# Row buffers, PSUM banks, product order and weight splits of a streaming encoder step

## The chip, the cores and the metric

The kernel runs on one core of one Trainium2 chip. The metric is the device time of one launch in microseconds (us). The kernel before takes 997.57 us, the median of three runs (997.35 to 997.97).

## The reference, cut to what matters

One layer of a hybrid encoder for 512 prompt tokens and 32 sample tokens (544 columns), model width 1024, all in float32:

```
h = rmsnorm(x, g1);  z = h @ w_in            # 1024 -> 8200 columns, split into
#   mq mk mv mo (mLSTM), mi mf, sb sc sx (short conv), dq dk dv (diff attention), gt (3 x 1024 gates)
ya = sigmoid(mo) * rmsnorm(mlstm(mq, mk, mv, mi, mf))
yb = sb * dwconv3(sc * sx)
yc = rmsnorm(diff_attention(dq, dk, dv, cache_k, cache_v)) * 0.8
x  = x + (sum_b sigmoid(gt_b) * (y_b @ w_branch[b])) @ w_out
up = rmsnorm(x, g2) @ w_up                   # 1024 -> 5632
upc = causal_dwconv3(up)
x  = x + (silu(upc[:2816]) * upc[2816:]) @ w_down
y  = rmsnorm(x, norm_f)
```

The outputs are y and the new states (k, v, C, n, m, and the last rows of both convolutions).

## The kernel before, in words

All tensors lie transposed, features on the 128 partitions and the 544 tokens along the free axis. Every large product is done in three passes of 272 columns: ScalarE (ACT) rounds a weight tile of 4 x 128 columns to `w_h` (`split`, L1019), VectorE (DVE) makes the rest `w_l` (`split`, L1315), and TensorE (PE) adds high x high, high x low and low x high. Such a weight tile is a unit. There are five slots for split units (NSPLIT), and the split of unit g + 4 (AHEAD) stands in the queues of ACT and DVE at the place of the block that multiplies with unit g.

The input projection works on pairs of 128-feature blocks: 30 pairs named (mq, 0), (mv, 0), ... (gt2, 3), in the list `pairs`. A pair's 2 x 2 block product (two feature blocks by two token halves) is formed with Strassen's scheme in seven products of 12 matmuls, called 1 to 7 (`strassen_product`, L1788). Products 1, 6, 7, 4 accumulate one after another in one PSUM bank (bank 0 or 2, in turn by pair), and after each of them the running sum is one output block. Product 2 has bank 1, products 5 and then 3 accumulate in bank 3. ACT copies the bank to the row buffer after 1, 6, 7 and 4 (L1141); DVE adds bank 1 after 2 and bank 3 after 5 and after 3 to what ACT copied ("merge", L1496). The next product in a bank waits until the sum before it has been read out. The merge of 5 stands in DVE's queue at the place of 7, since it adds to the block that ACT copies after 7. Some products use weight sums that DVE makes beforehand (`make_t`, L1335, L1339), at places counted back from their use.

The order of all work is one list, ORDER, built by a planner at the top; each engine walks through it and takes what is its own. A counter, `clock`, rises by one for each Strassen product and by two for each branch product. Small steps are hung on it by `at_time` and are put in the list when the clock has come so far: the mLSTM steps ("ml"), the attention steps ("at": scores s, row maximum mx on DVE, exponential ex on ACT, difference of the two maps wd on DVE, transposes t on PE, copy wt on ACT, product with the values o, output transpose y), and the steps after a pair ("post": tanh of a gate, the short convolution's u, w, c, the splits hi and lo of a branch's input). For a pair whose product 1 was already put inside the pair before, the order is 2, 6, 5, 7, next pair's 1, 4, 3. For gate pairs after a gate pair it is 1, 5, 6, 2, 7, branch product, 4, 3, branch product.

A branch product ("pr", 24 matmuls on L1729) multiplies a branch's input with `w_branch`; its two halves need two neighbouring banks, and it waits until DVE has drained the last user of both. DVE drains it with L1651, and adds it to `merged`. The banks are given by `project`: a pair's first branch product gets bank 1 and the chain bank that the pair doesn't use, the second bank 1 and the pair's own. After the last gate pair, and after (gt0, 3), two more branch products follow, in banks 0, 1 and then 2, 3.

Row buffers: the pairs mo, sx, sb and gt are copied to `tmp`, four rows, two for each pair, so two pairs at a time. `tmp_user` lists who must be done with a pair of rows before ACT's copy after product 1 may write it (`wait_tmp_free`). The pair (gt1, 0) follows (sb, 0) on the same rows, and (gt1, 1) follows (sb, 1).

After the branches come w_out (8 blocks "wo"), the second norm, 44 blocks "up" of the FFN with the convolution on DVE (`ups`, `acc`), and w_down ("dn", 6 units of 4 or 3 k-tiles for each output block). After the last "up" block ACT first waits for the last gated product, rounds it (`high_g`, L1028), and only then comes to the splits that stand at the place of the first "dn" block.

Of the kernel before, what the change touches and what calls it, by code (L numbers as in the profile page):

```python
# [50 lines left out]
def streaming_encoder_step(nc, x_prompt, x_sample, cache_k, cache_v, state_C, state_n, state_m, state_conv,  # L51
# [32 lines left out]
    pair_banks = {q: (2 * (i % 2), 1, 3) for i, q in enumerate(pairs)}  # L84
# [59 lines left out]
    def put(pair, w):  # L144
        prod(pair, w)
        if w == 3:
# [17 lines left out]
    pr_banks = {}  # L164
    for i, q in enumerate(pairs):
# [90 lines left out]
    merged_at = {q: max(n_of(q, 5), n_of(q, 7)) for q in pairs}  # L256
    for kind, a, n in ORDER:
        if kind == "p":
            pair, w = a
            if w in (1, 6, 7, 4):  # L260
                count["act"] += 1
                drained[n] = ("act", count["act"])
            if w in (2, 3) or n == merged_at[pair]:
                count["dve"] += 1
                drained[n_of(pair, 5) if n == merged_at[pair] else n] = ("dve", count["dve"])
# [28 lines left out]
    for kind, a, n in ORDER:  # L294
# [9 lines left out]
        else:  # L304
            for b in banks_of[n]:
                last_user[b] = n
# [66 lines left out]
    tmp_row, tmp_before, holder = {}, {}, [None] * 4  # L373
# [14 lines left out]
    for kind, a, n in ORDER:  # L388
# [10 lines left out]
        elif kind == "p" and a[1] == 1:  # L399
# [10 lines left out]
            elif q[0] == "gt1":  # L410
                tmp_user(q, "merged_added", 2 * q[1] + 2, rows=2)
# [7 lines left out]
    with ctx:  # L419
# [120 lines left out]
        u_c = at(28672, "u_c", [P, 2, TW + 2])  # L540
# [34 lines left out]
        for nm in (  # L575
# [27 lines left out]
                "x_used u_ready cu_ready conv_kept "  # L603
# [23 lines left out]
        def wait_tmp_free(eng, key):  # L627
            for name, v in tmp_before[key]:
# [5 lines left out]
        def tmp_pair(key):  # L634
            return tmp[:, tmp_row[key]:tmp_row[key] + 2, 0:T]
# [18 lines left out]
        def dst_of(pair, blk, half):  # L654
# [8 lines left out]
            return tmp[:, tmp_row[pair] + blk, cols]  # L663
# [73 lines left out]
        def units(n):  # L737
            return range(first_unit[n], first_unit.get(n + 1, len(UNITS)))

# [239 lines left out]
        def _(act):  # L979
# [56 lines left out]
            for kind, a, n in ORDER:  # L1036
                if n is not None:
                    for g in units(n):
                        if g + AHEAD < len(UNITS):
# [84 lines left out]
                elif kind == "p" and a[1] in (1, 6, 7, 4):  # L1124
                    q, w = a
                    blk, half = {1: (0, 0), 6: (1, 0), 7: (1, 1), 4: (0, 1)}[w]
# [144 lines left out]
                elif kind == "up":  # L1271
# [834 lines left out]
```

## Time and profile before

| what | value |
|---|---|
| median of 3 runs | 997.57 us |
| the profiled execution's own time | 997.3 us |
| its span | 995.5 us |
| PE busy | 971.8 us (98%) |
| DVE, ACT, POOL busy | 692.2, 472.6, 163.9 us |
| DMA, mean over the span | 100 GB/s |
| granted TensorE clock | 1.00 in the stages looked at |

The span is the profiler's, from the first to the last instruction; the time has 1.8 us more around it. A timeline row says start, duration, engine, line, operation and tiles, and in square brackets how long the engine had been idle before it and what released it. The end of a matmul is modelled and overlaps with the next one.

### The profile page before, as it was taken

The page shows a single profiled execution, that of the slowest core. Times are in us where ns is not written, and L with a number is a line of the kernel's source. Part 1 is how long each engine was busy: PE and PEld are TensorE (multiplying, and loading weights), DVE is VectorE, ACT ScalarE, POOL GpSimd, SP SyncE. Part 2 cuts the span into 40 slices and gives each one's busy share as a digit, 9 for nine tenths or more (in the row PEclk, how much of TensorE's full clock was granted, in tenths as well). Part 3 has the DMA queues.
Part 4 walks back from the last instruction along what each step waited for, and adds up shares of the span by engine and source line. Part 5 has one row for each costly group of instructions (what it writes and reads, how often), then busy time and mean ns, then how long its engine had stood idle before and what let it go on. Part 6 is the DMA issues. An engine that isn't in the chain of part 4 may idle for free.

```text
span 995.5 us, 20106 instructions
## 1 busy us (share of the span) xinstructions
PE 971.8 (98%) x7749; PEld 948.7 (95%) x7749; DVE 692.2 (70%) x1161; ACT 472.6 (47%) x982; POOL 163.9 (16%) x346
## 2 busy tenths in 40 slices
PE   7999999999999999999999999999999999999996
PEld 6999899999999998899999999999999999999996
DVE  6887666687667898777775557777777777634354
ACT  5675555576555665665554323333333333322242
POOL 2000121110121221021112212111111111111011
PEclk9999999999999999999999999999999999999999
DMA  6522243364231222223245212222222222332242
GB/s 197 196 85 86 72 112 108 91 210 135 66 86 43 86 86 85 65 86 107 64 129 174 86 45 91 93 93 93 91 92 86 86 86 80 120 97 81 81 147 97
DMA packets 104086, 99.87 MB, mean 100 GB/s; under 512 B 4868, under 2 KB 99481, under 8 KB 103735
## 3 DMA queue, kind: packets, MB, share of 16 engines
q1 hardware_dynamic: 98799, 85.51, 28.0%
q10 hardware_dynamic: 4072, 10.23, 2.9%
q0 software_dynamic: 1120, 2.86, 1.0%
q8 instruction: 62, 1.02, 0.4%
q14 instruction: 33, 0.27, 0.1%
HBM read 91.26 MB, written 7.31 MB: 99 GB/s over the span
## 4 chain that ended last, share of the span: by engine, by line
PE 85%; DVE 6%; ACT 4%; issue 3%; POOL 1%; DMA 0%; DVEq 0%; POOLq 0%; ACTq 0%
PE D L1729 46%; PE D L1788 28%; PE D L1748 2%; DVE w_l L1315 2%; ACT w_h L1019 1%; PE X L2023 1%; PE X L2061 1%; PE D L1760 1%; PE D L1873 1%; DVE ups L1685 1%; PE D L1915 1%; PE X L1969 1%; DVE acc L1695 0%; PE X L1970 0%; PE X L1972 0%
## 5 line engine op out<-in xcount | busy, mean ns | idle before, releaser
L1315 DVE TENSOR_TENSOR w_l<-raw,w_h 128x512 fp32r<-128x512 f32 (+1 forms) x286 | 200.8, 720 | 107.0 <-ACT w_h L1019 105.1
L1788 PE MATMUL D<-a_h,w_h 128*128 128x272 f32 x840 | 250.4, 298 | 2.9 <-DVE tmp L1496 1.5
L1788 PE MATMUL D<-a_h,w_l 128*128 128x272 f32 x840 | 243.1, 289 | 0.0
L1788 PE MATMUL D<-a_l,w_h 128*128 128x272 f32 x840 | 241.7, 288 | 0.0
L1019 ACT ACTIVATE w_h<-raw 128x512 fp32r<-128x512 f32 (+1 forms) x286 | 171.3, 617 | 97.3 <-PE D L1729 73.9
L1788 PEld LDWEIGHTS D<-a_h,w_h 128*128 128x128 f32 x840 | 158.1, 188 | 8.3 <-DVE tmp L1496 3.0
L1788 PEld LDWEIGHTS D<-a_l,w_h 128*128 128x128 f32 x840 | 158.4, 189 | 0.0
L1788 PEld LDWEIGHTS D<-a_h,w_l 128*128 128x128 f32 x840 | 158.0, 188 | 0.0
L1729 PE MATMUL D<-h_h,w_h 128*128 128x272 f32 x704 | 145.9, 288 | 0.0
L1729 PE MATMUL D<-h_h,w_l 128*128 128x272 f32 x704 | 145.7, 288 | 0.0
L1729 PE MATMUL D<-h_l,w_h 128*128 128x272 f32 x704 | 145.1, 288 | 0.0
L1315 DVE TENSOR_TENSOR w_l<-tw,w_h 128x512 fp32r<-128x512 f32 x120 | 83.9, 705 | 52.7 <-ACT w_h L1019 43.3
L1729 PEld LDWEIGHTS D<-h_h,w_h 128*128 128x128 f32 x704 | 110.6, 188 | 0.2 <-DVE ups L1685 0.2
L1729 PEld LDWEIGHTS D<-h_l,w_h 128*128 128x128 f32 x704 | 110.6, 188 | 0.0
L1278 ACT ACTIVATE acc<-ups,fcw 128x546 f32<-128x546 f32 x44 | 33.1, 753 | 162.6 <-POOL ffn_last L961 162.6
L1729 PEld LDWEIGHTS D<-h_h,w_l 128*128 128x128 f32 x704 | 109.9, 189 | 0.0
L1019 ACT ACTIVATE w_h<-tw 128x512 fp32r<-128x512 f32 x120 | 75.5, 630 | 42.7 <-PE D L1729 16.6
L1729 PE MATMUL D<-g_h,w_h 128*128 128x272 f32 x352 | 80.7, 290 | 0.7 <-DVE w_l L1315 0.7
L1729 PE MATMUL D<-g_h,w_l 128*128 128x272 f32 x352 | 79.8, 288 | 0.0
L1729 PE MATMUL D<-g_l,w_h 128*128 128x272 f32 x352 | 79.7, 287 | 0.0
L1688 DVE SCALAR_TENSOR_TENSOR acc<-ups,fcw,acc 128x546 f32<-128x546 f32 x44 | 34.7, 788 | 57.9 <-ACT acc L1278 57.9
L1729 PEld LDWEIGHTS D<-g_h,w_h 128*128 128x128 f32 x352 | 57.8, 188 | 1.3 <-DVE w_l L1315 1.0
(347 smaller groups left out, 1672.2 us busy)
## 6 DMA issues: line engine op xcount, KB each, us to landing
raw<-in_w_in SPq DMA_DIRECT2D x64, 512.0 KB, 4.3
raw<-in_w_up SPq DMA_DIRECT2D x44, 512.0 KB, 4.0
raw<-in_w_down SPq DMA_DIRECT2D x20, 512.0 KB, 3.8
raw<-in_w_branch SPq DMA_DIRECT2D x12, 512.0 KB, 3.5
raw<-in_w_out SPq DMA_DIRECT2D x8, 512.0 KB, 4.4
raw<-in_w_down SPq DMA_DIRECT2D x10, 384.0 KB, 3.4
x_spill<-xT ACTq DMA_DIRECT2D x1, 2176.0 KB, 7.4
xT<-x_spill ACTq DMA_DIRECT2D x1, 2176.0 KB, 10.0
```

What stands on the lines that cost most here:

```text
L1019: sc.activation(split_view(w_h, g), whole_view(g), ACT.Copy).then_inc(S["wh_ready"], 1)
L1278: sc.activation(acc[part][:, j % 2, 0:T + 2], ups[m % 2][:, 2:T + 4], ACT.Copy, scale=fcw[:, 2, jj:jj + 1])\
L1315: v.tensor_tensor(split_view(w_l, g), whole_view(g), split_view(w_h, g).bitcast(F32), ALU.subtract)\
L1685: last = v.tensor_tensor(to, d, r, ALU.mult)
L1688: link(v.scalar_tensor_tensor(out=ac, in0=u[:, 1:T + 3], scalar=fcw[:, 1, jj:jj + 1], in1=ac, op0=ALU.mult, op1=ALU.add))
L1729: last = t.matmul(banks(n)[:, half if at_bank is None else at_bank, 0:HALF], w[:, k, :], x[:, kx + k, HALF * half:HALF * half + HALF], sta ...
L1748: last = t.matmul(banks(n)[0:w.shape[2], half, 0:HALF], w[:, k, :], left_of(x, kx)[:, half, :], start=kx == 0 and i == 0, stop=kx == KD - ...
L1760: last = t.matmul(banks(n)[0:w.shape[2], half, 0:HALF], w[:, k, :], left_of(x, kx)[:, half, :], start=kx == 0 and i == 0, stop=kx == KD - ...
L1788: last = t.matmul(out, wt[:, k, :], x[:, left, k, :], start=w in (1, 2, 5) and k == i == 0, stop=k == KQ - 1 and i == 2, skip_group_check= ...
L1873: last = t.transpose(B[:, j // 4, P * (j % 4):P * (j % 4) + L], src[:, P * j:P * j + P], ident[0:L, 0:L])
L1915: last = t.transpose(B[:, P * c:P * c + P], src_tok(name, j)[:, P * c:P * c + P], ident[:])
L1969: t.matmul(o, qi[:, h, 0:L], C[:, h, :], start=True, stop=False)
```

## The change

- **Order of products.** A pair whose product 1 is already done, and that doesn't follow a gate pair, has 6, 2, 5, 7, next pair's 1, 3, 4. In it the roles of 5 and 7 on the last block are exchanged (`held` is 7): ACT copies 5, and DVE adds 7, in the place of 7. (sc, 0) has 1, 5, 6, 2. The first pair and the gate pairs keep their order.
- **gtr**, the transposes of the gate rows, moves from the pair (mq, 1), between 6 and 5, to (mv, 1), after 5. A pair's first `tok` transposes come after product 7 and not before it.
- **Banks.** From (sc, 0) on the chain banks 0 and 2 change places. At (gt0, 3) the second branch product takes banks 0, 1, and the two after it 2, 3 and 0, 1. At the end the product after (gt2, 3)'s two takes banks 4, 5, which the attention used before.
- **Third row buffer.** `tmp_c`, two rows in the place of `u_c` (the short convolution's buffer), holds (gt1, 0) and later (gt1, 3). The copy to it waits for the four convolution blocks (`taps_done`, new, `conv_kept`).
- **Splits.** The splits of units 4 and 5 of the first "dn" block are taken out of that block's place. ACT does the first behind the `acc` scaling of the last "up" block and the second ahead of the last `high_g`; DVE does the first behind the last convolution tap and the second behind the last gated product.

The diff, cut to its core:

```
-    pair_banks = {q: (2 * (i % 2), 1, 3) for i, q in enumerate(pairs)}
+    pair_banks = {q: (2 * ((i + (i > pair_no[("gt0", 3)])) % 2), 1, 3) for i, q in enumerate(pairs)}
...
         if prev == ("gt0", 3):
-            project(prev, 0, (0, 1), (0, 1))
-            project(prev, 1, (2, 3), (0, 1))
+            project(prev, 0, (2, 3), (0, 1))
+            project(prev, 1, (0, 1), (0, 1))
...
+        held[q] = 7 if started and not gated else 5
         if gated and not started:
             order = (5, 6, 2)
         elif prev == ("gt0", 3):
+            order = (5, 6, 2)
+        elif held[q] == 7:
             order = (6, 2, 5)
         else:
             order = (2, 6, 5)
         for w in order:
             put(q, w)
-            if q == ("mq", 1) and w == 6:
-                add("gtr", 0)
+        if q == ("mv", 1):
+            add("gtr", 0)
+        put(q, 7)
         for f in toks if i else []:
             f(prev, 0)
-        put(q, 7)
...
-        put(q, 4)
+        put(q, 3 if held[q] == 7 else 4)
         for f in toks:
             f(prev, 2)
-        put(q, 3)
+        put(q, 4 if held[q] == 7 else 3)
         if gated:
-            project(prev, 1, (min(a, 1), max(a, 1)), (1, 0) if a == 0 else (0, 1))
+            free = other if q == ("gt0", 3) else a
+            project(prev, 1, (min(free, 1), max(free, 1)), (1, 0) if free == 0 else (0, 1))
     last = pairs[-1]
     tick(1)
-    project(last, 0, (0, 1), (0, 1))
+    project(last, 0, (4, 5), (0, 1))
...
+    copied = {q: (1, 6, 12 - held[q], 4) for q in pairs}
...
-                tmp_user(q, "merged_added", 2 * q[1] + 2, rows=2)
+                tmp_user(q, "merged_added", 2 * q[1] + 2, rows=2, row=4 if q[1] in (0, 3) else None)
...
         def wait_tmp_free(eng, key):
+            if key == ("gt1", 0):
+                eng.wait_ge(S["taps_done"], 4)
+                eng.wait_ge(S["conv_kept"], 4)
...
+        EARLY = [first_unit[block_of[("dn", 0)]] + i for i in (0, 1)]
...
-                        if g + AHEAD < len(UNITS):
+                        if g + AHEAD < len(UNITS) and g not in EARLY:
                             split(g + AHEAD)
...  (ACT, "up")
+                    if a == (JF - 1, 1):
+                        split(EARLY[0] + AHEAD)
                     if part == 1:
                         act.wait_ge(S["conv_done"], up_index[(j, 0)] + 1)
...  (ACT, "last_g")
+                    split(EARLY[1] + AHEAD)
                     high_g(JF - 1)
...  (DVE, merge)
-                    wait_drained(dve, n_of(q, {2: 1, 3: 6}.get(w, 7)))
+                    wait_drained(dve, n_of(q, {2: 1, 3: 6}.get(w, 12 - held[q])))
...  (DVE, "up", behind conv_done and behind g_ready)
+                    if a == (JF - 1, 1):
+                        split(EARLY[0] + AHEAD)
...
+                    if a == (JF - 1, 1):
+                        split(EARLY[1] + AHEAD)
```

## Rows read from the trace of the kernel before

**Rows 1.** The profile's page, part 1: busy time, share, instructions of each engine.

```profile
PE 971.8 (98%) x7749; PEld 948.7 (95%) x7749; DVE 692.2 (70%) x1161; ACT 472.6 (47%) x982; POOL 163.9 (16%) x346
```

**Rows 2.** Windows: length, busy of PE, PEld, DVE, ACT, POOL, granted clock, DMA.

```profile
360.00:380.00 20.00, 19.59 (x153) 18.48 (x152) 19.68 (x40) 11.98 (x30) 3.12 (x9) 1.00 0.21 61
380.00:390.00 10.00, 8.91 (x65) 7.88 (x66) 8.06 (x18) 6.40 (x19) 2.16 (x5) 1.00 0.28 90
390.00:405.00 15.00, 12.58 (x95) 11.73 (x95) 12.00 (x20) 10.33 (x23) 2.50 (x5) 1.00 0.24 72
...
600.00:700.00 100.00, 100.00 (x800) 100.00 (x800) 77.63 (x124) 37.54 (x64) 19.84 (x59) 1.00 0.26 86
```

**Rows 3.** Waits of PE: who for whom, us in total, times, longest.

```profile
PE X L2044 <- DVE prob L1358: 2.6, 3, 1.1
...
PE D L1788 <- DVE tmp L1496: 1.5, 3, 0.8
```

**Rows 4.** Timeline of PE, the end of the branch products.

```profile
523.30 0.29 PE L1729 MATMUL D<-yc_h,w_l 128*128 128x272 f32 x1
524.45 0.37 PE L1729 MATMUL D<-yc_h,w_h 128*128 128x272 f32 x1 [0.86 <-DVE tmp L1651]
```

**Rows 5.** Timeline of PE, DVE and ACT, first down block.

```profile
860.50 0.52 PE L1729 MATMUL D<-g_h,w_h 128*128 128x272 f32 x2 [0.74 <-DVE w_l L1315]
...
855.17 1.90 DVE L1695 SCALAR_TENSOR_TENSOR acc<-tmp,acc 128x546 f32<-128x546 f32 x1
...
859.32 3.39 DVE L1315 TENSOR_TENSOR w_l<-raw,w_h 128x384 fp32r<-128x384 f32 x5 [1.43 <-ACT w_h L1019]
...
857.93 0.66 ACT L1028 ACTIVATE g_h<-acc 128x544 fp32r<-128x544 f32 x1 [3.22 <-DVE acc L1702]
```

**Rows 6.** Timeline of PE, single pauses at 162, 294 and 304 us.

```profile
162.30 0.39 PE L1788 MATMUL D<-a_h,w_h 128*128 128x272 f32 x1 [0.39 <-ACT dv_tok L1105]
...
294.95 0.37 PE L1729 MATMUL D<-ya_h,w_h 128*128 128x272 f32 x1 [0.42 <-DVE merged L1651]
...
304.88 0.39 PE L1788 MATMUL D<-a_h,w_h 128*128 128x272 f32 x1 [0.49 <-ACT scb L1141]
```

**Rows 7.** Timeline of PE, DVE and POOL, second mLSTM chunk.

```profile
132.87 0.35 PE L1969 MATMUL X<-C_p,qi 128*128 128x129 f32 x1 [0.88 <-DVE p_ml L1548]
...
128.59 0.69 DVE L1315 TENSOR_TENSOR w_l<-tw,w_h 128x512 fp32r<-128x512 f32 x1 [2.56 <-ACT w_h L1019]
129.19 1.96 DVE L1339 TENSOR_TENSOR tw<-raw,tw 128x512 f32<-128x512 f32 x1
...
129.53 1.07 POOL L875 TENSOR_TENSOR kw<-mk_tok,w_ml 128x512 f32<-128x512 f32 x1
```

**Rows 8.** Timeline of PE, ACT and DVE, attention step 8.

```profile
345.06 0.55 PE L2044 MATMUL X<-ident,prob 128*128 128x128 f32 x3 [1.13 <-DVE prob L1358]
...
337.92 0.40 ACT L1141 ACTIVATE scb<-D 128x272 f32<-128x272 f32 x1 [1.59 <-PE D L1788]
...
336.95 0.17 DVE L1624 COPY u_c<-vec 128x2 f32<-128x2 f32 x1
...
341.55 0.69 DVE L1315 TENSOR_TENSOR w_l<-tw,w_h 128x512 fp32r<-128x512 f32 x1 [2.36 <-ACT w_h L1019]
```

**Rows 9.** Timeline of PE and ACT, 380 to 405 us.

```profile
380.43 0.39 PE L1788 MATMUL D<-a_h,w_h 128*128 128x272 f32 x1 [0.84 <-DVE tmp L1496]
...
394.90 0.39 PE L1788 MATMUL D<-a_h,w_h 128*128 128x272 f32 x1 [0.28 <-DVE tmp L1496]
...
401.68 0.39 PE L1788 MATMUL D<-a_h,w_h 128*128 128x272 f32 x1 [0.41 <-DVE tmp L1496]
...
404.26 0.30 PE L2067 MATMUL X<-ident,on 128*128 128x128 f32 x1 [0.81 <-ACT wdT L1253]
...
383.36 0.40 ACT L1141 ACTIVATE tmp<-D 128x272 f32<-128x272 f32 x1 [2.14 <-DVE yb_l L1605]
...
398.05 0.40 ACT L1141 ACTIVATE tmp<-D 128x272 f32<-128x272 f32 x1 [2.14 <-DVE yb_l L1605]
```

More of the change, by code:

```diff
@@ L145, in put @@
         prod(pair, w)
-        if w == 3:
+        if w in (3, 4) and ("p", pair, 7 - w) in block_of:
             c = clock[0] + 1
@@ L164, in streaming_encoder_step @@
     pr_banks = {}
+    held = {}
     for i, q in enumerate(pairs):
@@ L259, in streaming_encoder_step @@
             pair, w = a
-            if w in (1, 6, 7, 4):
+            if w in copied[pair]:
                 count["act"] += 1
@@ L264, in streaming_encoder_step @@
                 count["dve"] += 1
-                drained[n_of(pair, 5) if n == merged_at[pair] else n] = ("dve", count["dve"])
+                drained[n_of(pair, held[pair]) if n == merged_at[pair] else n] = ("dve", count["dve"])
         elif n is not None:
@@ L305, in streaming_encoder_step @@
             for b in banks_of[n]:
-                last_user[b] = n
+                if kind != "pr" or b < 4:
+                    last_user[b] = n
     def units_of(kind, a):
@@ L539, in streaming_encoder_step @@
         junk = at(28160, "junk", [P, P])
-        u_c = at(28672, "u_c", [P, 2, TW + 2])
+        u_c, tmp_c = at(28672, "u_c", [P, 2, TW + 2]), at(28672, "tmp_c", [P, 2, TW])
         scb = at(80544, "scb", [P, 4, TW])
@@ L634, in tmp_pair @@
         def tmp_pair(key):
-            return tmp[:, tmp_row[key]:tmp_row[key] + 2, 0:T]
+            r = tmp_row[key]
+            return tmp[:, r:r + 2, 0:T] if r < 4 else tmp_c[:, :, 0:T]
         def bank(i):
@@ L662, in dst_of @@
                 return f_tmp[:, blk, cols]
-            return tmp[:, tmp_row[pair] + blk, cols]
+            return tmp_pair(pair)[:, blk, cols]
         def scale_of(pair):
@@ L1123, in _ @@
                         act.dma_start(y_p[0, 3 * P:4 * P, cols], yst[:, 3, cols]).then_inc(S["y_out"], 16)
-                elif kind == "p" and a[1] in (1, 6, 7, 4):
+                elif kind == "p" and a[1] in copied[a[0]]:
                     q, w = a
-                    blk, half = {1: (0, 0), 6: (1, 0), 7: (1, 1), 4: (0, 1)}[w]
+                    blk, half = {1: (0, 0), 6: (1, 0), 7: (1, 1), 5: (1, 1), 4: (0, 1)}[w]
                     act.wait_ge(S["dense_done"], n + 1)
@@ L1364, in _ @@
                     for g in units(n):
-                        if g + AHEAD < len(UNITS):
+                        if g + AHEAD < len(UNITS) and g not in EARLY:
                             split(g + AHEAD)
@@ L1493, in _ @@
                     dve.wait_ge(S["dense_done"], n + 1)
-                    wait_drained(dve, n_of(q, {2: 1, 3: 6}.get(w, 7)))
-                    out, src = dst_of(q, *{2: (0, 0), 3: (1, 0)}.get(w, (1, 1))), chain_bank(q, w if w in (2, 3) else 5)
+                    wait_drained(dve, n_of(q, {2: 1, 3: 6}.get(w, 12 - held[q])))
+                    out, src = dst_of(q, *{2: (0, 0), 3: (1, 0)}.get(w, (1, 1))), chain_bank(q, w if w in (2, 3) else held[q])
                     v.scalar_tensor_tensor(out=out, in0=src, scalar=scale_of(q), in1=out, op0=ALU.mult, op1=ALU.add)\
@@ L1631, in _ @@
                                                 op0=ALU.mult, op1=ALU.add))
-                    link(v.scalar_tensor_tensor(out=cu, in0=u[:, 2:T + 4], scalar=vec[:, 24 + j:25 + j], in1=cu,
-                                                op0=ALU.mult, op1=ALU.add))
+                    v.scalar_tensor_tensor(out=cu, in0=u[:, 2:T + 4], scalar=vec[:, 24 + j:25 + j], in1=cu,
+                                           op0=ALU.mult, op1=ALU.add).then_inc(S["taps_done"], 1)
+                    dve.wait_ge(S["taps_done"], j + 1)
                 elif kind == "post" and a[0][0] == "sb" and a[1] == "y":
@@ L1645, in _ @@
                     q = (f"gt{br}", j // 2)
-                    g = tmp[:, tmp_row[q] + j % 2, 0:T]
+                    g = tmp_pair(q)[:, j % 2, :]
                     dve.wait_ge(S["tanh_done"], th_no[q] + 1)
```

4 lines of the change are left out of this document (2 added, 2 removed).

## The prediction

> **What bounds the kernel now.** I read the page's busy times first, then windows, then the waits of PE, and then the timeline around each wait. PE is busy for 971.8 of 995.5 us [rows 1], and in a stretch of the up blocks it has no idle time: 800 matmuls in 100.00 us, 0.125 us each, at a granted clock of 1.00 [rows 2]. So the kernel is bound by PE, and no part of the change removes or adds a matmul. What it can win or lose is PE's pauses. Between 25 us and 990 us the trace has few: the waits of PE name two groups with several cases [rows 3], and the rest are single ones [rows 4 to 9]. The idle figure of a row is too small by a constant: from 523.30 to 524.45 us are 1.15 us where 0.125 is the normal step, so the pause costs 1.02 us where the row says 0.86 [rows 4]. The modelled end of a matmul covers the missing 0.16. I count each pause as its idle figure plus 0.16.
>
> Between 360 and 405 us the picture is another one. DVE is busy for 19.68 of 20.00 us, while PE still has 19.59 [rows 2]; from 380 on PE loses 1.09 us in 10 and 2.42 us in 15. There DVE is the engine that is late. The edit removes no work from DVE, so only pauses that come from the order of its work, or from DVE waiting for ACT, can go.
>
> **The change part by part.** All sums are against the profiled execution's own 997.3 us.
>
> *Bank 4, 5 at the end.* After (gt2, 3) the third branch product takes banks 0, 1 just after the second had bank 1, so it waits until DVE has drained it: 1.02 us [rows 4]. With banks 4, 5, whose last user is the attention, nothing is left to wait for; the product after it takes 2, 3, drained by then. What is late next would be the splits of `merged` for w_out; they are a chain behind the last branch product and move with it. Term: 1.02.
>
> *Branch products at (gt0, 3).* The same conflict, idle 0.42 [rows 6], so 0.58. In the new order each of the four products has a bank pair that was left one product (3 us) earlier. Term: 0.58.
>
> *(sc, 0) as 1, 5, 6, 2.* Before, 6 follows 1 in the same bank at once and waits for ACT's copy: 0.49 + 0.16 = 0.65 [rows 6]. With 5 between there are 1.5 us (12 matmuls of 0.125), and the copy takes 0.40 (the same operation in rows 8). Term: 0.65.
>
> *Tokens at (dv, 1).* Product 2 waits for ACT to read the token transposes out of bank 1: 0.39 + 0.16 = 0.55 [rows 6]. Between them stands one product before and two (4, 6) after. Term: 0.55.
>
> *Splits inside the last up block.* PE stands 0.74 us for the fifth unit of the first down block, until DVE's split that starts at 859.32; DVE waits for ACT, and ACT's splits are behind `high_g`, which starts at 857.93 after an idle time of 3.22 us [rows 5]. The cost is 0.74 + 0.16 = 0.90. After the change ACT can do the fifth unit's split in those idle 3.22 us, and DVE does it at about 855.2, when the last tap is done. The sixth comes at about 858.5 after the gated product. PE wants the fifth at 859.6 and the sixth 18 matmuls (2.3 us) later. DVE's and ACT's gated product is later by one split, 0.68 (3.39 / 5, rows 5), and its low part by POOL is needed some 3 us after the fifth unit's start; that is the cover, and without it the block would lose those 0.68 again. Term: 0.90.
>
> These five make 3.70 us, and each is a wait that the new order leaves without a cause. The next three are less sure.
>
> *Second mLSTM chunk.* PE stands 0.88 for `p_ml` (1.04 us in all) [rows 7]. In DVE's queue a weight sum of 1.96 us stands ahead of it, from 129.19. The sum for product 4 is placed six units ahead of product 4; as 4 becomes the last product, it moves one place back, behind `qi` and `p_ml`. So these can start after the split at 128.59, some 1.9 us earlier, if ACT's exponentials and POOL's `kw` are done (POOL's starts at 129.53 and takes 1.07, so it ends at 130.60, ahead of 131.8 when PE asks). Bounds 0 and 1.04, I take 0.90. The Trainium skill ("SBUF — State Buffer", section "Who interferes with whom") says that a DVE operation with two SBUF inputs is wholly blocked while a GpSimd operation that reads SBUF holds the shared port. The row of 1.96 us beside POOL's 1.07 agrees. By this rule `qi` and `p_ml`, which have one input in PSUM, are not held and the term would be the full 1.04; nothing else hangs on it.
>
> *ACT no longer copies 7.* At attention step 8 PE stands 1.13 (1.29 us) for DVE [rows 8]. DVE had been idle 2.36 us until ACT's split, and ACT had waited 1.59 us for product 7 to end before it went on at 337.92. In the new order ACT has copied 5 one place earlier and doesn't wait for 7; it can go on once `u_c` is there, at 337.12 [rows 8]. So its queue comes forward by 0.3 (the copy, net) to 0.8 us more, 1.1 in all, and DVE's with it. Bounds 0 and 1.29, I take 1.0.
>
> *The crowded stretch, 380 to 405 us.* Six pauses: three of L1788 [rows 9], two of L2044 (the row of rows 3 has 2.6 us in three cases, less the 1.13 of rows 8), one of L2067 [rows 9]. With 0.16 each they cost 1.00, 0.44, 0.57, 1.8 together, and 0.97. At 380.43 product 3, last of its pair, waits for DVE's merge in the place of 7. In the new order product 4 is last and waits for a merge in the same place, with as many products between: this pause stays. At 401.68 product 5 waits for DVE's merge of the pair before's 3; 3 is now one product earlier and one place earlier in DVE's queue: 0.57 go. The third row buffer takes away ACT's waits at 383.36 and 398.05, 2.14 us each [rows 9], as (gt1, 0) gets rows of its own and (gt1, 1) those that (sb, 0) left at 383. ACT's splits after them come earlier, DVE waits less for them, by less than 1 us each time. That covers the small pause at 394.90 (0.44) and half of the one at 404.26 (0.49). The two of L2044 are a chain of DVE, ACT and DVE again that the edit leaves alone. Term: 0.57 + 0.44 + 0.49 = 1.5, bounds 0.4 and 4.8 (all six).
>
> *Cost of what is added.* The wait for the four convolution blocks ahead of (gt1, 0)'s copy: behind it in ACT's queue stand the splits of the next units. The last tap is done by DVE before ACT comes to that copy, since in the rows ACT stood there for `yb_l` alone; nothing, against up to 2.14 if it came as late as the rows did. gtr costs PE the same at its new place. The new order has one tighter spot: product 6 waits for ACT's copy of 1, and between them stand 3, 4 instead of 4, 3, 2, so 3.0 us for 4.5. Where ACT is on time it copies within the 0.40 of its row; in the crowded stretch it can be late. Bounds 0 and 1.7 (one pause of the size of 0.57 in three crowded pairs), I take 0.7.
>
> **Sum.** 3.70 + 0.90 + 1.0 + 1.5 - 0.7 = 6.4 us, so 997.3 - 6.4 = 990.9 for the profiled execution. The median is 0.27 above that execution, so I predict 991.2. Nothing takes the gain back later: from 405 us on PE is the bound again, and a block that starts earlier ends earlier.
>
> **The rivals.**
> 1. *The stretch that DVE bounds gives nothing, the clean waits do.* For it: DVE's 19.68 of 20.00 us [rows 2]. Against it: DVE is idle in the pauses of 390 to 405 us (12.00 of 15.00). Only the five clean terms less 0.4: 997.57 - 3.3 = 994.3.
> 2. *All goes.* The moved merges let DVE catch up everywhere: 3.70 + 1.04 + 1.29 + 4.8 = 10.8, so 986.8. Against it: the pause at 380.43, whose cause isn't touched.
> 3. *Only the two pauses behind the crowded stretch count.* Whatever is won before 380 us meets a queue of DVE that cannot come earlier, since DVE is full from 360 on, and is lost as longer pauses there. Then 1.02 + 0.90 = 1.92, so 995.65, no change by my measure. Against it: DVE still waits for ACT at 341.55 [rows 8], so before 360 it has slack, and its queue moves with PE's progress.
> 4. *Slower.* ACT's copy of product 1 is now on PE's path. 18 pairs have the new order. If each waits 0.6 us there (ACT reaching the copy more than 3.0 us after the product, as at the two rows of 2.14 us), that is 10.8 us against 7.1 of gains, about 1001.3. It decides from about 3.5 us of lag of the copy behind the product's end in every pair; for it speaks only the crowded stretch, and there the third buffer removes what makes ACT late.
> That the change doesn't do what it says is possible for the buffer: with the convolution's taps late, the wait of 2.14 at 383.36 stays, which costs less than 1 us of the forecast and lies in its range.
>
> **How the numbers follow.** Forecast (988.8 to 993.5) 0.60; rival 1 0.20; rival 2 0.06; rival 3 0.08; rival 4 0.06. A measurement of this kernel tells 0.2%, 2.0 us, from no change. Forecast, rivals 1 and 2 are faster by more than that: 0.86. Rival 3 is the same: 0.08. Rival 4 is slower: 0.06. The range leaves out rivals 2, 3 and 4 (0.20): from 988.4 (the sum with the upper bounds of the chunk and of step 8, and halfway to that of the crowded stretch, 9.2) to 995.2 (the clean terms less the larger part of 1.7, 2.4).
>
> **What would show it.** Right: no pause of PE with L1729 at the end of the branch products and none in the first down block; no wait of ACT L1141 for `yb_l`; the pause for `p_ml` and the one of 1.13 for L2044 gone or under 0.3; the sum of PE's waits for DVE `tmp` down from 1.5 to about 0.8, with the one that stays on product 4 of (sb, 1); PE's busy time as before. Wrong: new rows of PE L1788 waiting for ACT L1141 of some tenths each, more than 1.5 us in all (rival 4), or pauses of L2044 that grow by what was won before 380 us (rival 3).

## The result, and the profile after

| kernel | median us | runs | ratio to before |
|---|---|---|---|
| before | 997.72 | 997.35 to 997.97 | |
| after | 992.60 | 992.01 to 993.25 | 0.9945 [0.9933, 0.9958] |

The change takes 5.1 us off, where 6.4 were forecast. The profiled execution took 993.04 us with a span of 991.2 us, against 997.3 and 995.5. PE is as busy as before [rows 1]; what went is pauses. Line numbers shift with every edit: a matmul of `strassen_product` is L1788 before, L1810 after and a few lines off in the experiments; operation and tiles tell which it is. First the busy times of the page of the kernel after, then the same four windows as in [rows 2].

```profile
PE 971.5 (98%) x7749; PEld 949.6 (96%) x7749; DVE 690.3 (70%) x1161; ACT 472.4 (48%) x982; POOL 162.8 (16%) x346
```

```profile
360.00:380.00 20.00, 18.40 (x143) 17.27 (x141) 19.65 (x42) 11.95 (x30) 3.12 (x9) 1.00 0.36 105
380.00:390.00 10.00, 8.93 (x66) 7.96 (x67) 8.96 (x17) 6.86 (x20) 2.87 (x5) 1.00 0.00 2
390.00:405.00 15.00, 14.45 (x114) 14.04 (x114) 12.92 (x22) 10.11 (x24) 2.36 (x5) 1.00 0.33 86
600.00:700.00 100.00, 100.00 (x800) 100.00 (x800) 78.03 (x124) 38.59 (x67) 19.45 (x56) 1.00 0.26 85
```

From 390 to 405 us PE now loses 0.55 us, and from 360 to 380 it loses 1.60, more than before. To see where time went, I took for each pair of blocks when its last matmul ended, before and after. PE's first pair ends 0.37 us earlier after, before any edit acts, so I take that off. What is left is an offset for each pair, after against before; the table has the steps from one offset to the next, which are what each stage gives (less than zero is time won).

| stage, up to the end of | step of PE's offset, us | what is there |
|---|---|---|
| (mv, 1) | +0.64 | new pause at gtr |
| (dk, 1) | +1.47 | granted clock 0.72 |
| (dv, 0) | -1.11 | pause for `p_ml` gone [rows 7] |
| (dq, 0) | +0.50 | new pause at 154.52 |
| (dv, 1) | -0.65 | tokens [rows 6] |
| (dq, 1) | +0.95 | new pause at 186.30 |
| last product of branch 0 | -0.69 | banks at (gt0, 3) [rows 6] |
| (sc, 0) | -0.75 | 1, 5, 6, 2 [rows 6] |
| (sx, 1) | -1.41 | step 8 [rows 8] |
| (sb, 0) | +1.20 | new pause at 366.40 |
| (gt1, 1) | -2.33 | crowded stretch [rows 9] |
| last branch product | -1.14 | banks 4, 5 [rows 4] |
| end of the down blocks | -0.7 | splits [rows 5] |

The new pauses of PE, as rows of its timeline after:

```profile
90.12 0.71 PE L1946 MATMUL D<-ident,rows 4*128 4x4 f32 x10 [0.58 <-DVE f_tmp L1513]
...
154.52 0.46 PE L1991 MATMUL X<-C_p,qi 128*128 128x129 f32 x2 [0.28 <-DVE p_ml L1565]
...
186.30 0.63 PE L2001 MATMUL X<-ident,qi 128*128 128x128 f32 x4 [0.80 <-DVE qi L1588]
...
366.40 0.30 PE L2089 MATMUL X<-ident,on 128*128 128x128 f32 x1 [1.03 <-ACT wdT L1267]
...
380.39 0.39 PE L1810 MATMUL D<-a_h,w_h 128*128 128x272 f32 x1 [0.97 <-DVE tmp L1513]
```

The last is no new one: it is the pause on product 4 of (sb, 1) that the prediction let stay. The pause at 186.30 is waiting for an output of DVE. In DVE's queue, after, a weight sum (L1356, 0.68 us) and a large one (L1352) now stand ahead of it:

```profile
181.74 1.22 DVE L1352 TENSOR_TENSOR tw<-raw 128x1024 f32<-128x1024 f32 x1
182.88 1.12 DVE L1581 SCALAR_TENSOR_TENSOR C_p<-C_p,il,X 128x129 f32<-128x129 f32 x4
183.92 0.68 DVE L1332 TENSOR_TENSOR w_l<-raw,w_h 128x512 fp32r<-128x512 f32 x1
184.52 0.68 DVE L1356 TENSOR_TENSOR tw<-tw,raw 128x512 f32<-128x512 f32 x1
185.12 0.43 DVE L1513 SCALAR_TENSOR_TENSOR dqT<-D,dqT 128x272 f32<-128x272 f32 x1
185.47 0.68 DVE L1588 TENSOR_TENSOR qi<-X,rr 128x512 f32<-128x512 f32 x1
```

One loss is none of DVE's. The next two rows are one window, of the kernel before and of the one after. The value behind the busy times is the granted clock: 1.00 before, 0.72 after.

```profile
112.00:118.00 6.00, 6.00 (x47) 5.41 (x46) 2.30 (x6) 1.49 (x5) 0.00 (x0) 1.00 0.01 3
```

```profile
112.00:118.00 6.00, 6.00 (x34) 5.24 (x34) 2.36 (x6) 0.76 (x2) 0.00 (x0) 0.72 0.01 3
```

In the same 6 us PE, busy all the time, got through 34 matmuls where it had been 47. From 114.11 to 117.2 us a matmul step is 0.227 us instead of 0.126, so PE ran at the lower of its two levels, 1.2 GHz, and at 2.4 before and behind. Ahead of it stand the small matmuls of the first mLSTM chunk, the same in both kernels. Thirteen steps at 0.10 us more are 1.3 us, most of the +1.47. It is not a fixed part of the new kernel: its executions lie at 992.01 and 992.15 us (mean granted clock 0.998), and at 993.04 and 993.25 (0.997 and 0.995); the profiled one is of the second kind. Executions of the kernel before that ran beside the experiments fall apart likewise, 997.5 to 998.4 us and 998.6 to 999.4, the latter nearly all at 0.995 or 0.996. Only one execution of each kernel has a trace, so this rests on the times and the mean clocks. So where less than 1.5 us is in question below, I compare stages in the profiles, or the fastest runs.

### The profile page after: what moved, and what is told of

Read it like the earlier page. It is cut to its first block, busy times and chain, and to the rows that moved or that the text cites. A ratio compares the mean times of both kernels' runs of the same rounds, so it can differ in the third digit from the quotient of the medians.

```text
span 991.2 us, 20106 instructions
## 1 busy us (share of the span) xinstructions
PE 971.5 (98%) x7749; PEld 949.6 (96%) x7749; DVE 690.3 (70%) x1161; ACT 472.4 (48%) x982; POOL 162.8 (16%) x346
## 3 DMA queue, kind: packets, MB, share of 16 engines
q8 instruction: 62, 1.02, 0.4%
## 4 chain that ended last, share of the span: by engine, by line
PE 90%; DVE 4%; issue 2%; ACT 2%; DMA 0%; POOL 0%; DVEq 0%; POOLq 0%; ACTq 0%
PE D L1751 51%; PE D L1810 28%; PE D L1770 2%; PE X L2045 1%; PE X L2083 1%; DVE w_l L1332 1%; ACT w_h L1033 1%; PE D L1782 1%; PE D L1937 1%; PE D L1895 1%; PE X L1991 1%; PE X L1992 0%; PE X L1977 0%; DVE tw L1352 0%; PE X L1994 0%
## 5 line engine op out<-in xcount | busy, mean ns | idle before, releaser
L1810 PE MATMUL D<-a_h,w_h 128*128 128x272 f32 x840 | 250.4, 298 | 1.4 <-DVE tmp L1513 1.0
L1810 PE MATMUL D<-a_h,w_l 128*128 128x272 f32 x840 | 243.6, 290 | 0.0
L1810 PE MATMUL D<-a_l,w_h 128*128 128x272 f32 x840 | 242.3, 288 | 0.0
L1810 PEld LDWEIGHTS D<-a_h,w_h 128*128 128x128 f32 x840 | 158.7, 189 | 5.6 <-issue 2.6
L1810 PEld LDWEIGHTS D<-a_l,w_h 128*128 128x128 f32 x840 | 159.1, 189 | 0.0
L1810 PEld LDWEIGHTS D<-a_h,w_l 128*128 128x128 f32 x840 | 158.6, 189 | 0.0
```

The source lines that it names most:

```text
L1810: last = t.matmul(out, wt[:, k, :], x[:, left, k, :], start=w in (1, 2, 5) and k == i == 0, stop=k == KQ - 1 and i == 2, skip_group_check= ...
```

## The experiments

Each is compared with the kernel before on the same chip, whose medians were 997.95 (e1 to e4), 998.38 (e5 to e8), 998.00 (e9 to e11) and 998.26 us (e12). Each of these four groups and the result ran at another time, and the kernel before differs by up to 0.4 us between e1 to e4 and e5 to e8, and by up to 0.7 from the result's 997.72. A difference of some tenths between runs of two groups is trusted only where the stages of the profiles show it too.

**e1, banks and splits alone.** The kernel before with the new banks at (gt0, 3) and behind (gt2, 3) and the splits inside the last up block; old order, two row buffers.

```
+    pair_banks = {q: (2 * ((i + (i > pair_no[("gt0", 3)])) % 2), 1, 3) ...
+    project(last, 0, (4, 5), (0, 1))
+    EARLY = [first_unit[block_of[("dn", 0)]] + i for i in (0, 1)]
```

> The kernel before with only the other banks at the branch ends and the splits inside the last up block. Theory A (swallowed): in the trace after, the pair (sb, 1) ends at 382.01 us as before (382.04), although pauses of 4.1 us ahead of it are gone; DVE is full between 345 and 380 us and sets that point. Then the 0.58 us won at (gt0, 3) are lost by (sb, 1), and the gain is 1.02 + 0.90 = 1.9 us. Theory B (additive): each removed pause counts by itself, and the change lost its early gains to new pauses of its own; then the gain here is 0.58 + 1.02 + 0.90 = 2.5 us and (sb, 1) ends 0.6 us earlier than before.

994.98 us (994.82 to 995.20), ratio 0.9968 [0.9955, 0.9980]: 3.0 us less, 2.50 by the prediction's terms. In its profile (gt0, 3)'s gain, 0.70 us, is still there at the ends of (sb, 1) and (gt1, 1). So a gain ahead of the stretch that DVE fills is not swallowed in it: theory B.

**e2, without the order.** The kernel after with the old order, roles, gtr and tokens; the third row buffer stays.

```
-        held[q] = 7 if started and not gated else 5
+        held[q] = 5
```

> The changed kernel with the product order, the roles of 5 and 7, the order of (sc, 0) and the place of gtr and of the tokens as before: buffer, banks and splits alone. If the third row buffer is what relieves the crowded stretch (2.5 us between the ends of (sb, 1) and (gt1, 1)), the time is the changed kernel's within 0.5 us: gain 1.9 + 2.5 = 4.4 us. If the order of products is, the stretch gives under 0.8 us and the gain is 1.9 to 2.7 us. My forecast had 0.57 of it on the order and 0.93 on the buffer: gain about 2.9 us.

993.62 us (993.43 to 994.91), 0.9956 [0.9944, 0.9969]. Its only edit over e1 is the buffer, worth 1.4 us, and the profile has it between (sb, 1) and (gt1, 1): 1.41. The kernel after has the new order on top of this and is only 1.0 us faster by the medians, 1.4 by the fastest runs: of some 5 us that the order wins in the stages, its costs eat 3.4.

**e3, without the buffer.** The kernel after, `tmp_c` and its wait taken out.

```
-                tmp_user(q, "merged_added", 2 * q[1] + 2, rows=2, row=4 if q[1] in (0, 3) else None)
+                tmp_user(q, "merged_added", 2 * q[1] + 2, rows=2)
```

> The changed kernel with two row buffers only: order, banks and splits. The complement of the run without the order. If the buffer relieves the crowded stretch: ACT waits for yb_l again twice (about 2 us each), (gt1, 1) ends within 0.5 us of before, gain 1.9 us. If the order does: gain 4 us or more. As forecast: 1.9 + 0.57 = 2.5 us.

993.33 us (992.92 to 994.54), 0.9952 [0.9939, 0.9966], about 0.9 more than after by the fastest runs, and 1.0 by the stages. PE has a pause that no other kernel has, here as a row of its timeline:

```profile
384.28 0.39 PE L1807 MATMUL D<-a_h,w_h 128*128 128x272 f32 x1 [1.61 <-ACT tmp L1152]
```

This is the mechanism of rival 4, product 6 waiting for ACT's copy of 1. It comes once, at (gt1, 0), and the third buffer removes it. Between the ends of (sb, 1) and (gt1, 1) the order alone wins 1.4 us here, as the buffer alone did in e2; together they win 2.46. So both expectations that named a single cause of the relief were met, and either edit gives more than half of it.

**e4, gtr behind product 7.** The kernel after with one line moved.

```
-        if q == ("mv", 1):
-            add("gtr", 0)
         put(q, 7)
+        if q == ("mv", 1):
+            add("gtr", 0)
```

> The changed kernel with the gate rows' transposes after product 7 of (mv, 1) instead of after 5. The trace after has a new pause of 0.58 (0.74 us in all) there, for DVE's merge of product 2, which has bank 1; with 5 and 7 between it should go. Theory A: nothing of it arrives, the time is the changed kernel's within 0.3 us and (sb, 1) ends as there. Theory B: 0.7 us faster than the changed kernel.

991.49 us (991.34 to 993.15), 0.9938 [0.9926, 0.9951]. The gtr pause is gone, and its 0.65 us are still there at the end of w_out. The fastest runs are 0.7 below those of after. The pause hung on the place of gtr between 5 and 7, where it waited for DVE's merge of product 2: theory B.

**e5, the weight sum of product 4 earlier.**

```
-                     (4, u_of(q, 4) - AHEAD - 2)):
+                     (4, u_of(q, 4) - AHEAD - 3)):
```

> The changed kernel with one edit: DVE makes the weight sum for product 4 of each pair one unit earlier in its queue (seven units ahead of the product and not six). Theory A (the pause before the last mLSTM chunk, 0.80 us at 186.3, and the small one at 154.5 come from that sum, which the new order of products moved in front of DVE's short mLSTM steps): both go, together -1.4 us at the end of pair (mo, 0), and the pause for p_ml at 132, which the new order had removed, comes back in part (0.3 to 1.0 us): net -1.1 to -0.1 us, no new pause elsewhere over 0.3. Theory B (these pauses come from the chain of ACT and DVE in the mLSTM chunk itself, whichever weight sum stands where): both stay within 0.3 us and 132 stays closed, 0.0 us.

992.71 us (992.01 to 993.23), 0.9943 [0.9930, 0.9957], no gain. The pause for `qi` at 186.3 fell from 0.80 to 0.33, but the one for `p_ml` near 133 us came back with 0.46: 0.48 us won at the first, 0.70 lost at the second. The small pause at 154.5 stays with 0.28. The sum in DVE's queue ahead of it (L1356 at 152.13 in after, 152.44 here) isn't the one that the edit moves. So theory A is right on the pause for `qi` and wrong on the small one. Two more stages changed. The pause of gtr at 90.12 is gone, 0.61 us won: the sum now fills idle time of DVE, from 85.36, and DVE's merge of product 2 ends earlier (it starts at 89.22, at 89.63 in after). And 0.44 us are lost by the end of (gt0, 1). The parts add up to next to nothing. e8, where gtr waits for nothing, shows the price of the earlier sum alone.

**e6, the order without the exchange of 5 and 7.** The order of after, but ACT copies 7 and DVE merges 5 in every pair.

```
-        held[q] = 7 if started and not gated else 5
+        held[q] = 5
+        late4 = started and not gated        # asked where held[q] == 7 was asked
```

> The changed kernel with the order of products kept, but with the old roles on the last block in every pair: ACT copies the chain's bank after 7, DVE merges 5 in the place of 7. Theory A (what closed the 1.13 us pause at attention step 8 is that ACT copies 5 and doesn't wait for 7): the pause between the ends of (sc, 0) and (sx, 1) comes back, 1.0 to 1.3 us later at (sx, 1) than the changed kernel, and ACT's idle time for PE at that copy is back over 1 us. Theory B (the moved products 3 and 4 and DVE's merges closed it, the role has no part): (sx, 1) ends within 0.3 us of the changed kernel, and the whole kernel takes the same within 0.5 us.

999.55 us (998.59 to 1001.96), 1.0013 [1.0003, 1.0022]: 7 us more than after, and a little more than before. Four of the pauses that it adds, as rows of PE's timeline:

```profile
71.45 0.39 PE L1811 MATMUL D<-a_h,w_h 128*128 128x272 f32 x1 [1.03 <-DVE f_tmp L1514]
...
236.56 0.48 PE L1811 MATMUL D<-a_h,w_h 128*128 128x272 f32 x1 [0.98 <-DVE tmp L1514]
...
370.89 0.39 PE L1811 MATMUL D<-a_h,w_h 128*128 128x272 f32 x1 [1.68 <-DVE tmp L1514]
...
385.86 0.39 PE L1811 MATMUL D<-a_h,w_h 128*128 128x272 f32 x1 [1.96 <-DVE tmp L1514]
```

There are six (also 0.18 and 0.57), all on product 3, 6.4 us of idle time. Product 3 takes bank 3 behind 5, and with the old roles DVE can read 5 out only when ACT has copied 7. One product then stands between 7 and 3, where the old order had two. Behind the last of them and behind the one at 236.56 the granted clock falls as well, each time for 14 matmuls, as two windows show (0.66, and 0.90 over a longer one).

```profile
386.00:391.00 5.00, 5.00 (x28) 5.00 (x29) 4.15 (x8) 2.99 (x10) 2.86 (x5) 0.66 0.00 0
...
224.00:240.00 16.00, 15.02 (x124) 12.30 (x124) 10.94 (x17) 8.19 (x15) 0.00 (x0) 0.90 0.50 162
```

And the pause of attention step 8 is back, with ACT idle for 1.59 us until product 7 has ended, as in [rows 8]: theory A.

```profile
348.64 0.55 PE L2067 MATMUL X<-ident,prob 128*128 128x128 f32 x3 [1.11 <-DVE prob L1376]
```

**e7, the convolution's scaling one product later.** The kernel of e4, and:

```
-                                  (2, "sx", "w0"), (3, "sx", "u1"), (4, "sx", "w1"),
+                                  (3, "sx", "w0"), (3, "sx", "u1"), (5, "sx", "w1"),
```

> The changed kernel with the gate rows' transposes after product 7 of (mv, 1) (as in the run before) and with ACT's scaling of the short convolution (scb from u_c) one product later, for both blocks of a pair. Theory A (before 390 us ACT's queue is held by this scaling, which stands waiting 2.71 and 1.24 us for a late DVE in pair (sx, 1); DVE then waits for ACT's splits, so the lateness is made by the two queues blocking each other): the pause for wdT at 366.4 (1.18 us) goes, those at 380.4, 384.4 and 398.1 shrink by 0.5 us or more together; 1.2 to 2.5 us less than with gtr alone, so 989.0 to 990.3. Theory B (DVE has too much work there, the order of ACT's does nothing): the ends of (gt1, 1) stay within 0.5 us of the run with gtr alone, 991.5; a pause that goes at 366 comes back behind it.

991.08 us (990.98 to 992.36), 0.9932 [0.9920, 0.9944], 0.36 below e4 by the fastest runs, 0.32 by the stages. The pause at 366.4 is gone, and 1.3 us are won by the end of (sb, 0). By the end of (sb, 1) 1.0 of them has been given back. First PE's row, then DVE's queue, where the first row and the last ones of its run without a pause stand:

```profile
378.39 0.39 PE L1810 MATMUL D<-a_h,w_h 128*128 128x272 f32 x1 [1.86 <-DVE tmp L1513]
```

```profile
355.56 0.69 DVE L1332 TENSOR_TENSOR w_l<-raw,w_h 128x512 fp32r<-128x512 f32 x1 [2.01 <-ACT w_h L1033]
...
374.20 0.77 DVE L1647 SCALAR_TENSOR_TENSOR scb<-u_c,vec,scb 128x546 f32<-128x546 f32 x1
375.01 0.79 DVE L1649 SCALAR_TENSOR_TENSOR scb<-u_c,vec,scb 128x546 f32<-128x546 f32 x1
375.83 0.69 DVE L1332 TENSOR_TENSOR w_l<-tw,w_h 128x512 fp32r<-128x512 f32 x1
376.44 0.95 DVE L1603 TENSOR_REDUCE nmax<-X 128x2 f32<-128x768 f32 x1
377.31 0.68 DVE L1332 TENSOR_TENSOR w_l<-tw,w_h 128x512 fp32r<-128x512 f32 x1
377.91 0.43 DVE L1513 SCALAR_TENSOR_TENSOR tmp<-D,tmp 128x272 f32<-128x272 f32 x1
```

The pause grew from 0.97 to 1.86. DVE had all its work and came only 0.3 us earlier, though PE was 1.3 ahead. Theory B holds here, for a gain made inside DVE's full stretch.

**e8, e7 with the earlier sum of e5.**

> The run before with the earlier weight sum of product 4 as well. If both parts act on stages of their own, its time is that of the run before plus what the weight sum alone does to the changed kernel, within 0.5 us. If DVE's queue in the stretch of 360 to 405 us is the bound, the earlier sum costs there again up to the 1.2 us that one late split takes.

992.01 us (991.61 to 993.19), 0.9939 [0.9926, 0.9951], 0.9 more than e7. In the profiles: 0.7 lost at `p_ml`, 0.5 won back at `qi`, 0.4 lost at (gt0, 1) and 0.2 more by (gt1, 1). The 0.61 that e5 won at gtr is in e7 already, so nothing stands against these losses.

**e9, one convolution tap less on DVE.** The kernel of e7 without the first of DVE's two taps in each of the four convolution blocks; two of the four taps left out, 1.56 us, stand ahead of the late merge. The short convolution's result lacks that tap.

```
-                    link(v.scalar_tensor_tensor(out=cu, in0=u[:, 1:T + 3], scalar=vec[:, 20 + j:21 + j], in1=cu,
-                                                op0=ALU.mult, op1=ALU.add))
```

> The run e7 with the first of DVE's two convolution taps left out (four instructions of 0.78 us, so the short convolution's result lacks one tap); two of them stand between 356 and 380 us. In e7's profile DVE runs without a pause from 355.56 to 378.34 us, and PE then waits 1.86 us for a merge at product 4 of (sb, 1). Theory A (from 356 us on DVE's own work is the bound, and this pause is its lateness): the pause shrinks by what is taken out ahead of it, 2 x 0.78 = 1.56, to 0.3 us, and the kernel takes 1.2 to 1.7 us less than e7, so 989.3 to 989.9. Theory B (the lateness is made by waits of DVE for ACT's splits, which come back when DVE is quicker): less than 0.6 us less than e7, and DVE shows new idle time before 378 us.

990.31 us (989.83 to 991.28), 0.9921 [0.9906, 0.9936]. PE's row:

```profile
378.76 0.39 PE L1808 MATMUL D<-a_h,w_h 128*128 128x272 f32 x1 [0.87 <-DVE tmp L1513]
```

1.0 less pause for 1.56 us less work; by the stages, with the clock fall of its profile taken out, it ends 1.2 us ahead of e7. DVE has one new wait for ACT (0.41 us at 367.44), so theory A holds for most of it and B for the rest (A had the pause at 0.3).

**e10, the merge ahead.** The kernel of e7 with one merge moved in DVE's queue; the second block's taps were meant to follow it.

```
+                if merges and a == (("sb", 1), 7):
+                    merge(n, *a)      # ahead of this block's split
-                                  (5, "sx", "c0"), (9, "sx", "c1") ...
+                                  (5, "sx", "c0"), (10, "sx", "c1") ...
```

> The run e7 with two moves inside DVE's queue and nothing taken out: at product 7 of (sb, 1) the merge stands ahead of the weight split, and the second block's convolution taps (1.56 us) come one product later. Theory A (PE waits there only for the place of the merge in a late queue, so the order can give back what the amount of work can't): the merge comes 0.6 + 1.6 = 2.2 us earlier, the pause of 1.86 is gone, 1.0 to 2.0 us less than e7, so 989.1 to 990.1, since some of DVE's lateness shows again at the attention's transposes at 383 and 396 us. Theory B (the whole lateness of DVE has to be paid somewhere): the pauses behind grow by as much, and the time stays within 0.4 us of e7.

991.16 us (990.50 to 991.77), 0.9930 [0.9918, 0.9943], the same as e7. The taps landed ahead of the merge all the same, so only the split's 0.6 us were tried: the pause is 1.26 instead of 1.86, and the next one, for the attention, 1.05 instead of 0.68, as the two rows show.

```profile
378.26 0.39 PE L1816 MATMUL D<-a_h,w_h 128*128 128x272 f32 x1 [1.26 <-DVE tmp L1339]
...
382.81 0.44 PE L2072 MATMUL X<-ident,prob 128*128 128x128 f32 x2 [1.05 <-DVE prob L1382]
```

Of 0.60 won at the first 0.37 are lost at the second, and by (gt1, 1) nothing is left: theory B, as far as it was tried.

**e11, the low part on POOL.** The kernel of e7, and:

```
+                elif kind == "post" and a[0][0] == "sb" and a[1] == "lo":       # POOL
+                    g.tensor_tensor(yb_l[:, js, :], tmp_pair(q), yb_h[:, js, :].bitcast(F32), ALU.subtract)
-                elif kind == "post" and a[1] == "lo":                           # DVE
+                elif kind == "post" and a[1] == "lo" and a[0][0] == "mo":
```

> The run e7 with the low part of the convolution branch's result (yb_l, two subtractions of 1.33 us on DVE at 380 and 394 us) on POOL. In the changed kernel's profile two pauses of PE stand behind these, 0.68 and 0.55 us plus 0.16 each, for DVE's difference of the attention maps. Theory A: both go and the time is 1.0 to 1.6 us less than e7, 989.5 to 990.1. Theory B (POOL's subtraction, about 1.4 us on 544 columns and so 2.7 on 1088, slows DVE as long as it runs, and DVE waited for ACT's splits anyway): less than 0.5 us.

995.01 us (993.32 to 995.27), 0.9966 [0.9954, 0.9979], 3.9 us more than e7 by the medians and 2.3 by the fastest runs. Its profile has the clock fall at 114 us, 1.5 us, which e7's doesn't; without it the rest is 3.2 by the stages. Neither theory foresaw a loss, but the mechanism that B names, DVE slowed while POOL subtracts, is what the rows show. The rows are POOL's, DVE's and PE's of one timeline:

```profile
375.25 2.54 POOL L923 TENSOR_TENSOR yb_l<-tmp,yb_h 128x1088 fp32r<-128x1088 f32 x1 [4.91 <-ACT yb_h L1174]
...
396.69 3.04 POOL L923 TENSOR_TENSOR yb_l<-tmp,yb_h 128x1088 fp32r<-128x1088 f32 x1
```

```profile
375.50 2.87 DVE L1653 SCALAR_TENSOR_TENSOR scb<-u_c,vec,scb 128x546 f32<-128x546 f32 x1
...
397.45 2.30 DVE L1379 SCALAR_TENSOR_TENSOR kap<-psum_p,rsum,neg_lam 128x1 f32<-128x1 f32 x1
```

```profile
381.80 0.59 PE L1816 MATMUL D<-a_h,w_h 128*128 128x272 f32 x1 [3.96 <-DVE tmp L1519]
```

The tap, 0.77 us in e7, takes 2.87 and ends 0.58 behind POOL's end: so DVE stood still until POOL had ended. PE's pause grew by the same 2.1 us, and behind it the granted clock was 0.50 for 5 us, the lower level, as the window of 381 to 386 us shows (18 matmuls):

```profile
381.00:386.00 5.00, 4.20 (x18) 4.20 (x19) 3.96 (x10) 4.43 (x13) 2.49 (x5) 0.50 0.00 0
```

So this pause cost more than itself: from the end of (sb, 0) to that of (sb, 1) PE loses 3.4 us against e7, where 2.1 are the pause. Each of the two subtractions took 1.33 us out of DVE's queue (their mean in e7) and put 2.1 us into it. The Trainium skill ("SBUF — State Buffer", "Who interferes with whom") states that a DVE instruction with two SBUF inputs contends with a GpSimd instruction that reads SBUF, and that the port pair they share is an exclusive lock; the trace agrees (2.87 against 0.77).

**e12, the split ahead of the exponentials.** The kernel of e7 with ACT's exponentials of attention step 9 and the copy `on` of step 8 behind the next product's split.

```
-                at_time(t0 + dt, "at", sub, u)
+                at_time(t0 + dt + {(9, "ex"): 0.9, (8, "on"): 1}.get((u, sub), 0), "at", sub, u)
```

> The run e7 with one step of ACT moved: the exponentials of attention step 9 and the output copy `on` of step 8 (1.30 us together at 353.85 us) stand behind product 6 of (sb, 0) and its weight split, no longer ahead of them. In e7 DVE is idle 2.01 us until that split (w_h at 354.79) and from 355.56 on runs without a pause until the late merge that costs PE 1.86 us at product 4 of (sb, 1). Theory A (DVE's lateness at 378 us is counted from the moment at which ACT releases it at 355): DVE's stretch begins 0.9 us earlier, the pause shrinks by as much, to about 0.9 us, and the kernel takes 0.7 to 1.0 us less than e7, so 990.1 to 990.4. Theory B (the lateness is set further on, by ACT's splits and DVE's moves inside the stretch): DVE starts earlier and pauses later, and the time stays within 0.3 us of e7's 991.08.

990.44 us (989.97 to 991.65), 0.9925 [0.9911, 0.9939], the fastest version that leaves nothing out: 7.8 us below before, 2.2 below after by the medians. DVE's row where its full stretch begins, and PE's where it pays:

```profile
354.93 0.69 DVE L1332 TENSOR_TENSOR w_l<-raw,w_h 128x512 fp32r<-128x512 f32 x1 [1.04 <-ACT w_h L1033]
```

```profile
377.90 0.39 PE L1810 MATMUL D<-a_h,w_h 128*128 128x272 f32 x1 [1.25 <-DVE tmp L1513]
```

DVE waits 0.97 us less at the beginning, and 23 us later PE's pause is 0.61 less. By the stages 0.10 us are won by the end of (sb, 0) and 0.72 more by that of (sb, 1), and nothing is lost behind it: 0.83 in all, 0.64 by the medians. Theory A.

## Why the prediction was right, and where it was not

The time is in the range, 1.4 us over the forecast. The gains came about where they were forecast and were larger, 8.9 us for 7.1; the costs were 3.4 for 0.7. That the sum is so near owes something to luck: two errors, 1.8 and 2.7 us, stand against each other.

*The five clean terms*, 3.70 forecast. Measured in the stages: 1.14 (forecast 1.02), 0.69 (0.58), 0.75 (0.65), 0.65 (0.55) and 0.7 (0.90), together 3.9. e1 shows three of them without the rest.

*Second chunk*, 0.90 forecast, 1.11 measured: the pause of [rows 7] is gone, and `qi` and `p_ml` start right behind the split, as foreseen. The sum's 1.96 us were mostly waiting for POOL: at its new place, 132.76 us, where POOL's `kw` is over, it takes 0.68, and e5, which puts it back, has 1.96 again. `p_ml`, with one input in PSUM, isn't held, as the prediction took it: 0.68 us from 131.54, beside POOL's `kw` from 131.21 to 132.28.

*Step 8*, 1.0 forecast, 1.41 measured. ACT's scaling that started at 338.21 before starts at 337.08, the 1.1 us foreseen. e6 shows the cause: with ACT copying 7 again the pause is back with 1.11. But this term was too narrow a reading of the exchange of 5 and 7. The prediction gave it 1.0 us at one place; e6 shows that without it the early product 3 pauses in six pairs, with two falls of the clock beside them, and all of the change's gain is lost.

*Crowded stretch*, 1.5 forecast, 2.46 measured from the end of (sb, 1) to that of (gt1, 1). The pause that was to stay stayed, with 0.97. Of 0.44, 0.57 and 0.97 for the three others in the prediction's list, 1.5 were taken, and all 1.98 are gone. The two for the attention, which I had said the edit leaves alone, went from 1.5 us of idle time to 0.68 and 0.55. ACT's two waits of 2.14 us for `yb_l` are gone, as foreseen. e2 and e3 give the buffer 1.4 us alone and 0.9 on top of the order. They also show that I shared it out wrongly. The pause at 401.68, which I gave to the order, is gone with the buffer alone (e2), and gone with the order alone (e3). The one at 404.26, half of which I gave to the buffer, stays with 0.81 in e2 and is down to 0.29 in e3: that is the order's. And the buffer alone takes the second attention pause from 0.92 to 0.56.

*Cost of what is added*, 0.7 forecast. This is the step that failed. I took gtr at nothing ("costs PE the same at its new place"); it costs 0.64, since it stands between 5 and 7 where its bank waits for DVE, and e4 gives that back; so does e5, by a weight sum that no longer delays that merge. I followed the weight sum of product 4 out of the way of `p_ml` and not to where it went: 0.95 at 186.30, of which e5 and e8 give back half by moving it. The 0.50 at 154.52 stays in both. Ahead of `qi` there stands another sum (152.13, 0.68 us), which before stood behind `p_ml` (152.28). It may be the cause, but no run moves it, and it isn't shown. And 1.20 at 366.40 hang on ACT, whose queue stands for the convolution; e7 shows that one. Together 3.3 us, and 0.13 more at (sb, 1). The wait that I had named instead, product 6 for ACT's copy of 1, doesn't occur.

*The granted clock*, in no term: 1.47 in the profiled execution, and by their times and mean clocks less or nothing in the fastest ones.

The sum by stages is 8.9 of gains, 3.4 of costs and 1.5 of clock: 4.0, and with the 0.37 by which the two profiles differ at the start about the 4.3 of the spans. The fastest runs differ by 5.3, the medians by 5.1.

*The rivals.* Rival 1 falls: the crowded stretch gave 2.46. Rival 2 falls, the pause at 380 stays. Rival 3 falls with e1, whose early 0.70 us cross the stretch whole. But its mechanism is real where a gain is made after DVE has begun to be full, at 355 us: e7 won 1.3 us at 366 and lost 1.0 by 378. What did count there was less work on DVE (e9) and an earlier beginning (e12). Rival 4 had one case, in e3.

*Open.* Why the clock falls in some executions and not in others was not tried by itself: it was seen at 112 to 118 us in six of the eleven profiles with the new order (after, e3, e4, e5, e9, e11), and in none of the three with the old one, but executions of before show a low mean clock too, at a place that no profile caught. e6 has two falls elsewhere, behind pauses, and e11 one. The pause at 154.52 is open too. What e10 meant to try, the merge ahead of the taps, stays untried.

## What to carry to other kernels

When a small step or a weight sum is moved in a queue, follow it to its new place and ask what short, urgent step now stands behind it; the pause that it leaves is half of the account. Find where the late engine's run without a pause begins: what PE won ahead of that point stayed won, of 1.3 us won inside 1.0 were given back at the next hand-over, and what paid there was work taken off that engine, or an earlier beginning. A role that looks like a detail of the new order, here which product waits for which copy, can be what carries it.

## What the runs showed of the hardware

- The granted clock can fall for 3 us in a stretch in which PE is never idle: 0.227 us a matmul instead of 0.126, behind 24 small matmuls, 1.3 to 1.5 us in all, in six of eleven profiles of nearly the same program. Behind pauses it fell too: behind 3.96 us in e11 (0.50 over 5 us) and in e6 behind 1.96 us (0.66 over 5 us) and behind 0.98 us at 236.56 (0.66 over 236 to 241 us). But it stayed at 1.00 behind 1.86 us in e7 (378 to 384 us) and in e6 behind 1.68 us at 370.89 (370 to 376 us) and 1.03 us at 71.45 (71 to 76 us). The length of the pause alone doesn't tell which.
- POOL reading two SBUF operands can stop DVE outright: a tap of 0.77 us, both tensors in SBUF, took 2.87. `p_ml`, one tensor in SBUF and one in PSUM, took its usual 0.68 beside POOL's `kw`. A tiny DVE operation of 128 x 1 elements with its first input in PSUM (`kap`, 0.22 us elsewhere) took 2.30 in e11, as long as POOL's subtraction went on; its other two operands, one of them the per-partition scalar, are in SBUF.
